# One core, two transformer blocks: x in four loads, a 16-column norm in the convolution, and four weight casts two units later

## The reference

```python
def swiglu(x, wg, wu, wd):
    return (jax.nn.silu(x @ wg) * (x @ wu)) @ wd
...
x = layer_norm(ALPHA * x + 0.5 * swiglu(x, ffn1_wg[l], ffn1_wu[l], ffn1_wd[l]), ln_f1_g[l], ln_f1_b[l])
```

```python
mu = jnp.mean(yf, axis=-1, keepdims=True)
var = jnp.mean(jnp.square(yf - mu), axis=-1, keepdims=True)
yn = ((yf - mu) * lax.rsqrt(var + EPS)).reshape(B, S, CONV_CH)
yn = yn * gn_g.astype(jnp.float32) + gn_b.astype(jnp.float32)
return jax.nn.silu(yn).astype(dt)
...
a = p[:, :, 0] - lam * p[:, :, 1]
return jnp.einsum('bhqk,bhkv->bhqv', a.astype(vh.dtype), vh)
```

## Time and profile before

| | us |
|---|---|
| three runs | 3096.06, 3098.64, 3100.68 |
| profiled execution | 3099.62 |
| its span | 3097.8 |
| TensorE busy | 2930.5 (95%) |
| VectorE busy | 1528.9 (49%) |
| ScalarE busy | 1210.8 (39%) |
| GpSimd busy | 1159.2 (37%) |
| TensorE's first matmul | 24.79 |

### The profile page before, as it was taken

How to read it: one execution, slowest core, us unless ns; L and a number is a source line. 1 busy time by engine, 2 the same in 40 slices (tenths; PEclk the granted TensorE clock), 3 DMA queues, 4 the chain that set the end, 5 groups by cost and what they waited for, 6 DMA issues and landing times.

```text
span 3097.8 us, 37812 instructions
## 1 busy us (share of the span) xinstructions
PE 2930.5 (95%) x13531; PEld 2338.1 (75%) x13531; DVE 1528.9 (49%) x2662; ACT 1210.8 (39%) x1843; POOL 1159.2 (37%) x598
## 2 busy tenths in 40 slices
PE   6999999889999999999999998899999999898997
PEld 5888878657788888888888765778888877675665
DVE  4442364445654423444145544564442579557665
ACT  3332232556343322433223355534332252535553
POOL 3445342421354444444435242145444343112221
PEclk9999999999999999999999999999999999899998
DMA  4333232201423332233323210242333221115995
GB/s 132 95 95 107 90 120 65 83 18 39 139 82 96 100 107 83 82 95 97 110 85 118 83 52 18 62 129 84 100 95 110 74 72 62 35 62 212 349 351 201
DMA packets 118541, 324.13 MB, mean 105 GB/s; under 512 B 12432, under 2 KB 48656, under 8 KB 117904
## 3 DMA queue, kind: packets, MB, share of 16 engines
q1 hardware_dynamic: 108992, 305.17, 30.4%
q10 hardware_dynamic: 2800, 8.91, 0.8%
q0 software_dynamic: 6624, 8.41, 0.8%
HBM read 313.52 MB, written 24.64 MB: 109 GB/s over the span
## 4 chain that ended last, share of the span: by engine, by line
PE 80%; DVE 12%; ACT 3%; issue 3%; POOL 1%; DMA 1%; DVEq 0%; SPq 0%; ACTq 0%; another core or an unknown queue 0%; POOLq 0%
PE ps L429 18%; PE ps L432 18%; PE ps L430 18%; PE ps L464 4%; PE ps L2041 3%; PE ps L993 2%; PE ps L2027 1%; PE ps L2029 1%; PE ps L2028 1%; PE ps L891 1%; DVE cacc L2344 1%; PE ps L536 1%; PE ps L491 1%; PE ps L487 1%; PE ps L488 1%
## 5 line engine op out<-in xcount | busy, mean ns | idle before, releaser
L2780 POOL TENSOR_TENSOR wlo<-raw,whi 128x1024 fp32r<-128x1024 f32 (+1 forms) x368 | 952.4, 2589 | 1478.6 <-ACT whi L591 1478.5
L591 ACT ACTIVATE whi<-raw 128x1024 fp32r<-128x1024 f32 (+1 forms) x368 | 409.3, 1113 | 745.1 <-PE ps L432 661.3
L429 PE MATMUL ps<-xlo,whi 128*128 128x512 f32 x1704 | 666.2, 391 | 7.0 <-DVE sg L1370 4.8
L430 PE MATMUL ps<-xhi,wlo 128*128 128x512 f32 x1704 | 663.7, 389 | 0.0
L432 PE MATMUL ps<-xhi,whi 128*128 128x512 f32 x1704 | 420.8, 389 | 0.0
L429 PEld LDWEIGHTS ps<-xlo,whi 128*128 128x128 f32 x1704 | 320.4, 188 | 76.4 <-POOL wlo L2780 7.0
L430 PEld LDWEIGHTS ps<-xhi,wlo 128*128 128x128 f32 x1704 | 320.4, 188 | 65.8
L432 PEld LDWEIGHTS ps<-xhi,whi 128*128 128x128 f32 x1704 | 319.9, 188 | 66.4
L429 PE MATMUL ps<-hlo,whi 128*128 128x512 f32 x704 | 277.3, 394 | 0.0
L430 PE MATMUL ps<-hhi,wlo 128*128 128x512 f32 x704 | 275.5, 391 | 0.0
L723 DVE SCALAR_TENSOR_TENSOR xa<-ps,xa 128x512 f32<-128x512 f32 x48 | 33.1, 689 | 367.5 <-PE ps L432 367.5
(11 more groups left out here) (610 smaller groups left out, 4881.7 us busy)
## 6 DMA issues: line engine op xcount, KB each, us to landing
raw<-in_gu SPq DMA_DIRECT2D x176, 512.0 KB, 3.5
raw<-in_mix SPq DMA_DIRECT2D x96, 512.0 KB, 3.6
mraw<-in_w SPq DMA_DIRECT2D x23, 2048.0 KB, 12.5
raw<-in_dn SPq DMA_DIRECT2D x64, 704.0 KB, 4.0
mdraw<-in_w SPq DMA_DIRECT2D x23, 1024.0 KB, 13.1
raw<-in_w SPq DMA_DIRECT2D x32, 512.0 KB, 3.5
gate_rows<-tails SPq DMA_DIRECT2D x32, 256.0 KB, 4.3
sgmn<-gate_rows SPq DMA_DIRECT2D x16, 512.0 KB, 4.0
```

The costliest lines, as they stand in the source:

```text
L429: nc.tensor.matmul(out, whi[:, slot, cols], rlo, start=first and t == 0, stop=False)
L430: nc.tensor.matmul(out, wlo[:, slot, cols], rhi, start=False, stop=False)
L591: nc.scalar.activation(whi[:, s, 0:n], raw[:, r, 0:n], ACT.Copy).then_inc(hi_done, 1)
L2780: nc.gpsimd.tensor_tensor(wlo[:, s, 0:n], raw[:, r, 0:n], whi[:, s, 0:n].bitcast(F32), ALU.subtract).then_inc(w_ready, 1)
```

## The change

The start: x comes in four quarters, and the loads of weight blocks 0 and 1 stand behind the first and the second. `xhi` is made by ScalarE, in turn with the weight casts; the constants are loaded behind that. TensorE begins without the constants, on the half of x and the parts of the weights that come first, and takes all products with `xlo` last. The convolution's norm averages each group once: 8 small matmuls give 16 columns of variances (4 tiles of tokens, 2 halves of 2 groups), one root and one reciprocal are taken of 16 columns, two copies spread them to 64 columns each, and at units 8 to 11 TensorE turns them back beside the scores, where VectorE scales straight from the bank. The bias goes into the sigmoid and the last product. The four output weight casts move from units 2, 6, 10, 14 to 4, 8, 12, 16. In the finish one tensor_scalar becomes a tensor_tensor.

```diff
+    def pe_start_pair(pe):
+        def add(b, w, x, k):
+            first, last = w is whi and x is xhi and k == 0, w is whi and x is xlo and k == KT - 1
+            ins = nc.tensor.matmul(ps[b][:], w[:, b, k * P:k * P + P], x[:, k, :], start=first, stop=last)
+            if last:
+                ins.then_inc(w_free, 1)
+        half = KT // 2
+        pe.wait_ge(hi_done, 1)
+        for k in range(half):
+            pe.wait_ge(norm_hi, k + 1)
+            add(0, whi, xhi, k)
+        pe.wait_ge(w_ready, 3)
+        for k in range(half):
+            add(0, wlo, xhi, k)
+        pe.wait_ge(hi_done, 2)
+        for k in range(half):
+            add(1, whi, xhi, k)
+        for k in range(half, KT):
+            pe.wait_ge(norm_hi, k + 1)
+            for b in range(2):
+                add(b, whi, xhi, k)
+        for k in range(half, KT):
+            add(0, wlo, xhi, k)
+        pe.wait_ge(w_ready, 4)
+        for k in range(KT):
+            add(1, wlo, xhi, k)
+        for k in range(KT):
+            pe.wait_ge(x_ready, k + 1)
+            for b in range(2):
+                add(b, whi, xlo, k)
...
+        if ver == 0:
+            pe_start_pair(pe)
+            pe.wait_ge(const_in, 32)
...
+                if extra:
+                    extra(u)
...
-        if u in (2, 4):
-            k = u // 2 - 1
-            pe.wait_ge(S["sq_ready"], k + 1)
-            if k:
-                pe.wait_ge(S["var_copied"], 1)
-            nc.tensor.matmul(ps[7][:], c("blk64"), rs2[:, k, :], start=True, stop=True).then_inc(S["stat_used"], 1)
+        if u == 2:
+            pe.wait_ge(S["sq_ready"], 2)
+            for k in range(2):
+                for kt in range(QT):
+                    ins = nc.tensor.matmul(ps[7][:, 8 * k + 2 * kt:8 * k + 2 * kt + 2], rs2[:, k, kt * P:(kt + 1) * P],
+                                           c("blk64")[:, 0:128:64], start=True, stop=True)
+            ins.then_inc(S["stat_used"], 1)
...
+    def pe_conv(pe, u):
+        if CONV_AT + 2 <= u < CONV_AT + 6:
+            pe.wait_ge(S["conv_scaled"], u - CONV_AT - 1)
+        if CONV_AT <= u < CONV_AT + 4:
+            out, k, cols = conv_piece(u)
+            if u == CONV_AT:
+                pe.wait_ge(S["conv_wide"], 2)
+            for i in range(2):
+                at_ = cols.start + P * i
+                nc.tensor.matmul(out[:, P * i:P * i + P], rs2[:, k, at_:at_ + P], ident, start=True, stop=True)
...
-        if u == 5:
-            act.wait_ge(S["var_copied"], 1)
-            nc.scalar.activation(rs2[:, 0, :], rs2[:, 0, :], ACT.Sqrt, bias=eps_ap(RMS_EPS)).then_inc(S["std_ready"], 1)
-            act.wait_ge(S["stat_used"], 2)
-            nc.scalar.activation(rs2[:, 1, :], ps[7][:], ACT.Sqrt, bias=eps_ap(RMS_EPS)).then_inc(S["std_ready"], 1)
+        if u == 3:
+            act.wait_ge(S["stat_used"], 1)
+            nc.scalar.activation(conv_r, ps[7][:, 0:16], ACT.Sqrt, bias=eps_ap(RMS_EPS)).then_inc(S["std_ready"], 1)
...
-            hi(act, B2, G2_OUT + n, 0, 8)
+        if u % 4 == 0 and 4 <= u <= 16:
+            hi(act, B2, G2_OUT + u // 4 - 1, 0, 8)
...
-            act.wait_ge(S["own_cq"], 1)
-            nc.scalar.activation(conv_sig[:], cacc[:], ACT.Sigmoid).then_inc(S["sig_ready"], 1)
+            act.wait_ge(S["conv_scaled"], 4)
+            for k in range(2):
+                nc.scalar.activation(conv_sig[:, k, :], cacc[:, k, :], ACT.Sigmoid, bias=p2("cnb", k)).then_inc(S["sig_ready"], 1)
...
+        if u == 4:
+            dve.wait_ge(S["std_ready"], 1)
+            own.link(nc.vector.reciprocal(conv_r, conv_r))
             own.wait()
+        if u in (5, 6):
+            k = u - 5
+            nc.vector.tensor_copy(rs2[:, k, :].rearrange("p (a c) -> p a c", c=64),
+                                  conv_r[:, 8 * k:8 * k + 8].unsqueeze(2).broadcast_to([P, 8, 64])
+                                  ).then_inc(S["conv_wide"], 1)
+        if CONV_AT <= u < CONV_AT + 4:
+            bank, k, cols = conv_piece(u)
             dve.wait_ge(S["norm_dve"], 2)
+            nc.vector.scalar_tensor_tensor(out=cacc[:, k, cols], in0=cacc[:, k, cols], scalar=p2("cng", k),
+                                           in1=bank, op0=ALU.mult, op1=ALU.mult).then_inc(S["conv_scaled"], 1)
+        if u == OG_AT + 3:
+            dve.wait_ge(S["sig_ready"], 2)
+            dve.wait_ge(S["conv_scaled"], 4)
             for k in range(2):
...
+                own.link(nc.vector.scalar_tensor_tensor(out=cacc[:, k, :], in0=cacc[:, k, :], scalar=p2("cnb", k),
+                                                       in1=conv_sig[:, k, :], op0=ALU.add, op1=ALU.mult))
...
-            own.link(nc.vector.tensor_scalar(w2[:, :, 1], w2[:, :, 1], small[:, 4:5], None, ALU.mult))
+            own.link(nc.vector.tensor_tensor(w2[:, :, 1], w2[:, :, 1], small[:, 4:5].broadcast_to([P, 2]), ALU.mult))
...
+        first = mk("gu1", 0, 8, W_FFN_UP)
+        x_pair(0)
+        first(0, G_FFN1, 0, 0)
+        x_pair(1)
+        first(0, G_FFN1, 0, 1)
+        x_pair(2)
+        x_pair(3)
+        for j in range(2, 4):
+            first(0, G_FFN1, 0, j)
...
-        pe.wait_ge(const_in, 32)
...
+        def x_hi(h):
+            act.wait_ge(x_in[h], 16)
+            for m in (2 * h, 2 * h + 1):
+                nc.scalar.activation(xhi[:, m, :], xa[:, m, :], ACT.Copy).then_inc(norm_hi, 1)
+        x_hi(0)
+        hi(act, 0, 0)
+        x_hi(1)
+        hi(act, 0, 1)
+        x_hi(2)
+        x_hi(3)
         act.dma_start(con[:], d["con"]).then_inc(const_in, 16)
         act.dma_start(par_all[:], d["par"].rearrange("l p c -> p l c")).then_inc(const_in, 16)
-        for b in range(3):
-            hi(act, 0, b)
+        hi(act, 0, 2)
         act.wait_ge(const_in, 32)
...
+        dve.wait_ge(start_own, 3)
+        dve.sem_inc(S["tile_free"], 2)
         for m in range(KT):
-            if m % 4 == 0:
-                dve.wait_ge(x_in[m // 4], 16)
-            nc.vector.tensor_copy(xhi[:, m, :], xa[:, m, :]).then_inc(start_own, 1)
-            dve.wait_ge(start_own, 4 + m)
-            dve.sem_inc(norm_hi, 1)
+            dve.wait_ge(norm_hi, m + 1)
             nc.vector.tensor_tensor(xlo[:, m, :], xa[:, m, :], xhi[:, m, :].bitcast(F32),
                                     ALU.subtract).then_inc(x_ready, 1)
```

More of the change, by code:

```diff
@@ L319, in program @@
     const_in = sem("const_in")
-    x_in = [sem("x_in0"), sem("x_in1")]
+    x_in = [sem(f"x_in{k}") for k in range(4)]
     go_pe, go_act = sem("go_pe"), sem("go_act")
@@ L368, in program @@
               "kl_ps": "o_ready", "kl_rows": "o_used", "u_ps": "kpe_copied", "states_ready": "cw_ready",
-              "o_ps": "ckv_n", "lam_sum": "rotated", "lam_exp": "kpe_copied", "late_out": "cmp_scored",
+              "conv_wide": "r_sum", "conv_scaled": "own_cq", "o_ps": "ckv_n", "lam_sum": "rotated", "lam_exp": "kpe_copied", "late_out": "cmp_scored",
               "z_sig": "cmp_exp", "q_std": "cmp_out", "k_std": "kc_ready", "k_r": "gate_back0", "k_r_ps": "gate_back1",
@@ L493, in pe_first_pair @@
                     ins.then_inc(w_free, 1)
+    def pe_start_pair(pe):
[28 more added lines that the diff above has]
+                add(b, whi, xlo, k)
     UP_BANK = (0, 1, 3, 4)
     def pe_ffn(pe, L, g, ver, last=False):
-        pe_first_pair(pe, L, g, lambda k: pe.wait_ge(norm_hi, ver * KT + (k + 1)),
-                      lambda k: pe.wait_ge(x_ready, ver * KT + (k + 1)))
+        if ver == 0:
+            pe_start_pair(pe)
+            pe.wait_ge(const_in, 32)
+        else:
+            pe_first_pair(pe, L, g, lambda k: pe.wait_ge(norm_hi, ver * KT + (k + 1)),
+                          lambda k: pe.wait_ge(x_ready, ver * KT + (k + 1)))
         for j in range(2, 4):
@@ L855, in program, with pe_units_whole @@
     s2_ring = [s2_sb[:, 0, :], s2_sb[:, 1, :], zs[:]]
-    def pe_units_whole(pe, units, bank_of, p, s_ring, ready=None, feed=None):
+    def pe_units_whole(pe, units, bank_of, p, s_ring, ready=None, feed=None, extra=None):
         n = len(units)
@@ L1702, in pe_second @@
         sync_point(pe, "pe", lambda: pe_late_products(pe, 0, LATE_FIRST))
-        pe_units_whole(pe, dif_units, dif_bank, pt2, s2_ring, feed=lambda u: pe_late(pe, u))
+        pe_units_whole(pe, dif_units, dif_bank, pt2, s2_ring, feed=lambda u: pe_late(pe, u), extra=lambda u: pe_conv(pe, u))
         for b in range(4):
@@ L1866, in pe_late, with conv_piece @@
                 ins.then_inc(S["gla_turned"], 1)
+    CONV_AT = 8
+    conv_r = stat[:, 112:128]
+    def conv_piece(u):
+        k, half = divmod(u - CONV_AT, 2)
+        return ps[2 + u % 2][:, 256:512], k, slice(256 * half, 256 * half + 256)
+    def pe_conv(pe, u):
[8 more added lines that the diff above has]
+                nc.tensor.matmul(out[:, P * i:P * i + P], rs2[:, k, at_:at_ + P], ident, start=True, stop=True)
     def act_late(act, u):
@@ L1910, in dve_late @@
```

(26 more changed lines are left out.)

2 lines of the change are left out of this document (1 added, 1 removed).

## The result

The changed kernel took 3078.24 us (median of 10 runs, 3073.93 to 3090.78); the kernel before, on the same chip, 3097.35 (10 runs, 3094.7 to 3112.41). The ratio is 0.9935, 95% interval 0.992 to 0.995: 15.5 to 24.8 us less. The forecast was 3079.

The account below looks back on a forecast made before the run. TensorE was taken as the bound, four fifths of the chain. Start -16.5, attention +1.2 and -5.5 made -20.8 on 3099.62 us, giving 3079; own range 3074 to 3084, with rivals and run spread 3071 to 3089.

Parts of the forecast that it names:

- The start: First 38 us: new order of loads, casts and matmuls brings the third weight block at 21.5 instead of 38.0, gain 16.5.
- the 4.8 us of the lower clock: At the start: TensorE's slow period after idling, counted from 9.3 us, when its work has no more gaps.
- the upper bound of 17.7: Start's largest gain: lower clock counted from the first matmul at 6.8, so it ends 2.5 us sooner.
- rival 2: At the start, the six loads don't overlap, each needing 3.6 us alone: gain 7.7, time 3088; chance 0.06.
- Rival 4: The start is held by late constants or weight block 3, cover of 3 us eaten: 3081 to 3084; chance 0.06.
- The attention up to unit 15: Added matmuls +0.9 and +1.9, new waiting at units 5 and 6 +0.8, old waits gone -2.4: sum +1.2.
- the three old waits: TensorE's attention waits of 1.14, 0.61 and 0.69 us for ScalarE's copy of softmax weights, expected to go: -2.4.
- rival 3: In attention, the clock falls at units 2 to 6 and stays down until 2685: slower, 3107.5; chance 0.03.
- From unit 15: Later attention: 3.3 us of wait and the clock's fall behind it go, 2.2 taken for the clock: -5.5.
- rival 1: Start gains, attention doesn't: splits meet other VectorE instructions, or ScalarE's sigmoids bring a clock fall at unit 20; 3084; chance 0.22.
- The move, not the swap: In the attention's finish, moving the weight casts must take the stall away; the changed opcode was costed at nothing.
- The prediction's own sign against it: Attention forecast is wrong if TensorE still waits some 4 us at unit 16, or the stage is no shorter.

Follow-up runs that it names:

- after_again: The changed kernel, unedited, run and profiled a second time: 3078.89 us.
- att: The kernel before with only the change's attention edits (convolution norm, moved casts, swap), on the old start: 3093.77 us, ratio 0.9985 to the kernel before.
- x_first: The changed kernel with x's four loads and casts ahead of those of the weight blocks: 3075.63 us.
- start_pair: The changed kernel with TensorE's old order at the start, waiting for both weight blocks whole: 3095.86 us.
- no_swap: The changed kernel with the tensor_scalar back in the finish: 3089.14 us, ratio 0.995 to the kernel before.
- casts_back: The changed kernel with the four output weight casts back at units 2, 6, 10 and 14: 3086.64 us, ratio 0.9958 to the kernel before.
- casts_only: The kernel before with only the four output weight casts moved two units later: 3096.29 us, ratio 0.9987 to the kernel before.
- start: The kernel before with only the change's edits to the loads and the first work of the engines: 3085.43 us, ratio 0.9949 to the kernel before.

## Why the prediction was right

**The start: right, a little short.** The predicted steps and the measured: first matmul 6.8 and 6.85; splits ended 9.3 and 11.8, measured 9.25 and 12.05; the wait for the low part ended at 9.3 both times; third block 21.5 and 20.37; gain 16.5 and 17.64 (17.0 in the slowest of the nine profiles). The term that was off is "I count the 4.8 us of the lower clock from 9.3, where its work has no gap any more". It ran from the first matmul, as the upper bound of 17.7 had it, over a wait that was only 0.22 us long. The loads came as laid out: the casts that they release start at 4.45, 5.74, 7.08 and 8.36, 1.3 apart, so rival 2 is out. By the fixed part that the Trainium skill gives in "DMA: Bandwidth & Descriptors", Anatomy of one DMA, they would, one after another, be an estimated 3.2 apart; the rows show no such part for queued loads. Rival 4 is out too: block 3's split ended at 22.69, wanted at 20.37 + 5.4, so 3.1 us of cover, and the low parts of x, the last done at 17.21, kept nobody waiting.

**The attention up to unit 15: +1.2 forecast.** Without a fall, unit 15 (by the start of its scores) came 39.2 us after unit 0 (after_again, att, x_first) against 39.5 before: -0.3. The added terms were about right (the sixteen passes 1.95 us for 2.0, the wait ahead of them 0.70 for the second square's 0.6), the three old waits went, and at units 5 and 6, where 0.8 was booked, after_again has none above 0.15. With the fall at unit 2 it was 44.8: +5.3. The step that failed there stands under rival 3: "I expect none above 0.5 there", although the same forecast books 0.6 for the second square at unit 2. The wait was 0.72, and the clock fell behind it in three of seven profiles. Its price was mis-sized the other way: 5.6 us (44.8 less 39.2), not 21.3, for it ended after 13.65 us.

**From unit 15: -5.5 forecast.** Measured without a long fall -6.9 (63.25 to 56.31, att; 56.29 in x_first), in the first profile -5.6, in after_again +0.1, in start_pair +4.3 and in no_swap +10.2. Of "3.3 of the 3.93 us wait" 2.8 went. The long fall behind it did not go for good, as the forecast had it; it came back behind unit 17 or 21 in three of the six profiles. So the term holds for an execution without a long fall, and its size on the whole is not shown. The new wait of 2.14 us at unit 21 is ScalarE's cost there, seen in rival 1.

**The move, not the swap, takes the stall away: right**, by casts_back and casts_only. That the swap is worth nothing in time is not shown (no_swap). The Trainium skill has the rule in "SBUF — State Buffer", Who interferes with whom: an instruction of VectorE with two SBUF inputs contends with one of GpSimd that reads SBUF, one with a single SBUF input outside VectorE's two-port modes does not. The rows agree on both halves: beside the stalls above, the new scaling, which reads one SBUF tensor and a bank, took its 0.47 us inside a split. The changed kernel's timeline:

```profile
2646.50 2.40 POOL L2835 TENSOR_TENSOR wlo<-raw,whi 128x1024 fp32r<-128x1024 f32 x1 [9.13 <-ACT whi L627]
...
2647.36 0.47 DVE L1982 SCALAR_TENSOR_TENSOR cacc<-cacc,par,ps 128x256 f32<-128x256 f32 x1
```

**The sum.** -20.8 forecast, -20.1 measured. By run time the parts gave 15.8 (start, 16.5 forecast) and 4.6 (att, 4.3 forecast), each with some 4 us of interval: that the sum comes out within 1 us is in part luck. The start's share has its mechanism in the traces. The attention's is a mean over stages of 95.5 to 118.3 us, not a saving that each execution has. The prediction's own sign against it, a stage no shorter than before, is there in two of the six profiles outright (112.4 and 118.3) and within 0.4 us in two more (102.4 and 102.5, for 102.8). The first profile has rival 1's outcome, and after_again something near its mechanism too, a fall of 17.1 us where ScalarE keeps TensorE waiting at unit 21.

What stays open: which wait the clock falls behind in a given execution, whether the norm gains anything on its own, and why no_swap ran longer.

## What to carry to other kernels

At a start that waits for transfers, interleave the loads in the order in which the products need them, and let the first products run on what is there: here leaving out either cost some 4 us of 17.6. Where VectorE's small instructions on two SBUF operands stand beside GpSimd's long ones, move the long one's release out of the way; here another opcode on the same operands stalled as long (2.22 us in casts_back, 2.12 in the earlier trace rows). And before crediting a stage with a few us, profile the same kernel several times and count the time at the lower clock in each: here the stage of programs alike but for one opcode ran from 95.5 to 118.3 us, a wider spread than the 20.1 us of the whole change, while the two profiles of the changed kernel itself happened to agree within 0.1.

## What the runs showed of the hardware that was not expected

TensorE's clock can stay at its lower level while TensorE is busy nearly all the time: 54.21 of 54.70 us in no_swap, at 0.50. And the same instructions with the same waits (1.1 us at unit 17, 2.1 at unit 21) were followed by 54.6 us of it, by 30.7 (start_pair), by 17.1, by 3.4 or by none. At the start, where the matmuls stand some 0.43 us apart instead of 0.23, the view of the changed kernel gives a clock of 1.00:

```profile
6.85:11.36 4.51, 4.29 (x9) 2.74 (x10) 3.62 (x2) 3.67 (x6) 4.23 (x2) 1.00 0.97 351
```

That is no measurement: the trace has no entry for the granted clock before 11.36 us, about where the spacing changes. In all fourteen traces the first entry stands within 0.2 us of the change of spacing (29.59 us in the kernel before). So for the start the spacing of the matmuls is the only witness of the lower clock.
